# Recurrences' set-up issued in the last chunk of z; first weight chunk split in the first stage, five copies issued in z's second chunk

## The reference

```python
h = _rmsnorm(x, prm['norm_pre_mix'][l])
z = h @ prm['w_in'][l]                      # (rows, 1024) @ (1024, 3740)
(rq, rk, rv, rg, mq, mk, mv, mi, mf, mo, gqkv, ga, gbeta, gg, nq, nkv, ngate) = jnp.split(z, IN_SPLITS, axis=-1)
o_ret, ret_S = _retention(...)              # three recurrences over the prompt
o_ml, ml_C, ml_n, ml_m = _mlstm(...)
gconv, gdn_conv = _causal_dwconv(st['gdn_conv'], gqkv, prm['gdn_conv_w'][l])   # width 4
gq, gk, gv = jnp.split(jax.nn.silu(gconv), 3, axis=-1)
o_g, gdn_S = _gated_delta(...)
```

## Time and profile before

| what | value |
|---|---|
| runs shown | 4123.53 us median of 3 (4115.71 to 4125.43) |
| profiled execution, its own time | 4113.04 us |
| its span | 4111.3 us |
| mean granted TensorE clock | 0.946 |
| busy: PE, DVE, ACT, POOL | 89%, 46%, 31%, 10% |
| matmuls of z, both layers | L565, L569, L570: 433.4, 384.5, 384.1 us busy (pipelined) |

### The profile page before, as it was taken

One profiled execution on the slowest core, in us unless ns is written; L12 is line 12 of the kernel. 1 busy time (PEld: TensorE's weight loads), 2 busy tenths in 40 slices (PEclk: granted clock), 3 DMA queues, 4 the chain that ended last, 5 costly groups with the idle time before them and its releaser, 6 DMA issues. The chain is left out here.

```text
span 4111.3 us, 55178 instructions
## 1 busy us (share of the span) xinstructions
PE 3677.8 (89%) x22004; PEld 3151.8 (77%) x22004; DVE 1908.6 (46%) x3752; ACT 1260.1 (31%) x2863; POOL 411.4 (10%) x287
## 2 busy tenths in 40 slices
PE   5999697698979999999979996967798999999998
PEld 3888587446668999997768885854465799999875
DVE  3234487663444333335541336875533543333345
ACT  2111265452222212124331113645422321121333
POOL 0035101002100000000000550010021100000000
PEclk9999799798989999999989997978898999999999
DMA  7344332306332222255542433332252422222653
GB/s 241 130 145 148 100 110 83 103 7 221 161 123 90 65 75 64 76 189 192 199 156 92 165 129 110 99 96 58 90 213 94 152 64 78 62 78 62 231 180 134
DMA packets 304475, 499.98 MB, mean 122 GB/s; under 512 B 66757, under 2 KB 228325, under 8 KB 299632
## 3 DMA queue, kind: packets, MB, share of 16 engines
q1 hardware_dynamic: 298955, 421.21, 32.1%
q0 software_dynamic: 4608, 67.11, 4.0%
q10 hardware_dynamic: 656, 8.13, 0.6%
HBM read 395.16 MB, written 116.52 MB: 124 GB/s over the span
## 5 line engine op out<-in xcount | busy, mean ns | idle before, releaser
L1042 PE MATMUL ps<-h_hi,fu_hi 128*128 128x344 f32 x2112 | 682.3, 323 | 10.1 <-DVE h_lo L1266 7.3
L1044 PE MATMUL ps<-h_hi,fu_lo 128*128 128x344 f32 x2112 | 677.5, 321 | 0.0
L1043 PE MATMUL ps<-h_lo,fu_hi 128*128 128x344 f32 x2112 | 677.1, 321 | 0.0
L565 PE MATMUL ps<-zi_whi,h_hi 128*128 128x468 f32 (+1 forms) x1152 | 433.4, 376 | 49.6 <-DVE zi_wlo L646 49.6
L1042 PEld LDWEIGHTS ps<-h_hi,fu_hi 128*128 128x128 f32 x2112 | 398.1, 188 | 14.1 <-DVE h_lo L1266 7.8
L1044 PEld LDWEIGHTS ps<-h_hi,fu_lo 128*128 128x128 f32 x2112 | 398.8, 189 | 0.0
L1043 PEld LDWEIGHTS ps<-h_lo,fu_hi 128*128 128x128 f32 x2112 | 398.2, 189 | 0.0
L569 PE MATMUL ps<-zi_wlo,h_hi 128*128 128x468 f32 (+1 forms) x1024 | 384.5, 375 | 0.0
L570 PE MATMUL ps<-zi_whi,h_lo 128*128 128x468 f32 (+1 forms) x1024 | 384.1, 375 | 0.0
L1068 PE MATMUL ps<-fd_whi,fd_fhi 128*128 128x512 f32 x704 | 276.6, 393 | 15.0 <-DVE fd_flo L1283 14.2
L565 PEld LDWEIGHTS ps<-zi_whi,h_hi 128*128 128x128 f32 x1152 | 217.6, 189 | 79.2 <-DVE h_lo L642 50.8
(11 more groups left out here) (624 smaller groups left out, 6736.4 us busy)
## 6 DMA issues: line engine op xcount, KB each, us to landing
w_ahead<-w_ffn_down SPq DMA_DIRECT2D x44, 1024.0 KB, 5.5
z<-zi_z SPq DMA_DIRECT2D x112, 234.0 KB
zi_h<-z SPq DMA_DIRECT2D x64, 384.0 KB, 4.6
f_all<-fu_f SPq DMA_DIRECT2D x44, 516.0 KB, 3.3
w_ahead<-w_ffn_gate SPq DMA_DIRECT2D x44, 512.0 KB, 4.8
w_ahead<-w_ffn_up SPq DMA_DIRECT2D x44, 512.0 KB, 6.1
fd_raw<-w_ffn_down SPq DMA_DIRECT2D x22, 1024.0 KB, 5.7
zi_raw<-w_in SPq DMA_DIRECT2D x24, 936.0 KB, 5.5
```

Source lines behind the costliest of these rows:

```text
L565: nc.tensor.matmul(out, rows_hi, w_hi[:, i % 2, k, c0], start=(k == 0), stop=False)
L1042: nc.tensor.matmul(out, up_hi[f % 2][:, j, k, :], h_hi[:, k, seg], start=(k == 0), stop=False)
L1043: nc.tensor.matmul(out, up_hi[f % 2][:, j, k, :], h_lo[:, k, seg], start=False, stop=False)
L1044: m = nc.tensor.matmul(out, up_lo[f % 2][:, j, k, :], h_hi[:, k, seg], start=False, stop=(k == KD - 1))
```

## The change

1. *First stage.* The four loads of the first weight chunk (first layer only) are issued by SP behind the third tile's store; ScalarE and VectorE make their halves at the end of the stage. `project_in` of the first layer no longer does this (`SPLIT`). For it the weight buffers get fixed places (`PromptEarly`).
2. *Copies.* The five copies leave ScalarE's queue and the first stage; SP issues them in z's second chunk, ahead of the store of tile 11.
3. *Set-up.* All of it moves into z's last chunk (tiles 63 to 71, `FINAL` = 63) in both layers; the first row tile's operands and first rows are loaded there too. The last chunk's tiles use six PSUM banks, the set-up two.
4. *Convolution.* Its steps stand four tiles apart, not five.

```diff
+                    if t == 2:
+                        for k in range(0, KD, 2):
+                            first_weights(sp, io, 0, E, k, S(f"w_first{k // 2}"))
...
-                act.wait_ge(S("row_stored"), 16)
-                norm_stored(kit, act)
-                for h in range(H):
-                    act.dma_start(env["wdist"][h], env["wrow"][h].partition_broadcast(P)).then_inc(env["first_copies"], 16)
-                act.dma_start(x_cur[0:SEQ, :], io["x_prompt"][0]).then_inc(env["first_copies"], 16)
+                for k in range(KD):
+                    if k % 2 == 0:
+                        act.wait_ge(S(f"w_first{k // 2}"), 16)
+                    nc.scalar.activation(E.w_hi[:, k], E.raw[:, k], ACT.Copy).then_inc(S("first_high"), 1)
...
+                for k in range(KD):
+                    dve.wait_ge(S("first_high"), k + 1)
+                    V.tensor_tensor(E.w_lo[:, k], E.raw[:, k], E.w_hi[:, k].bitcast(F32), ALU.subtract)
...
-    conv_in = {29 + 5 * j: j for j in range(NT)}
-    conv_act = {33 + 5 * j: j for j in range(NT)}
-    conv_scale = {34 + 5 * j: j for j in range(NT)}
+    SPLIT = KD if l == 0 else 0
+    conv_in = {29 + 4 * j: j for j in range(NT)}
+    conv_act = {32 + 4 * j: j for j in range(NT)}
+    conv_scale = {33 + 4 * j: j for j in range(NT)}
+    FINAL = (NZ - 1) * TT
...
+        return n % NBK if n < FINAL else (n - FINAL) % 6
...
+                        if l == 0 and n == TT + 2:
+                            first_copies(sp, env, io)
...
+                        if n == FINAL - 1:
+                            sp.wait_ge(S("lo_ready"), KD * NZ - SPLIT)
+                            setup.tables(sp)
+                            for k in range(NZO):
+                                sp.wait_ge(S(f"z_stored{k}"), 16 * len(range(k, FINAL, NZO)))
+                            setup.gate_columns(sp)
+                            sp.wait_ge(S("x_stored0"), 16)
+                            sp.wait_ge(S("z_summed"), FINAL)
+                            setup.first_heads(sp)
+                        if n == FINAL + 5:
+                            setup.rows_out(sp, 0)
+                        if n == FINAL + 6:
+                            setup.rows_back(sp, 0)
+                        if n == FINAL + 7:
+                            setup.rows_out(sp, 1)
+                setup.rows_back(sp, 1)
+                setup.all_in(sp)
...
+                        if n == FINAL + 2:
+                            z_wait(pe, users[6][-1])
+                            setup.pe_sums(pe)
+                        if n == FINAL + 3:
+                            z_wait(pe, users[7][-1])
+                            setup.pe_rows(pe)
+                        if n == FINAL + 4:
+                            setup.pe_max(pe)
+                        if n == FINAL + 5:
+                            setup.pe_ends(pe)
+                        if n == FINAL + 7:
+                            setup.pe_mu(pe)
...
+                    if n == FINAL + 1:
+                        setup.dve_gates(dve, link)
+                    if n == FINAL + 2:
+                        setup.dve_decays(dve, link)
+                    if n == FINAL + 3:
+                        setup.dve_scan(dve, link)
+                    if n == FINAL + 4:
+                        setup.dve_max(dve, link)
+                        setup.dve_shifts(dve, link)
+                    if n == FINAL + 7:
+                        setup.dve_rows(dve, link)
...
+    def pe_sums(self, pe):
+
+        S, T, R, ps = self.kit.sem, self.kit.nc.tensor, self.R, self.env["ps"]
+        pe.wait_ge(S("lf_g"), 1)
...
+    def dve_gates(self, dve, link):
...
+        dve.wait_ge(S("gates_in"), self.ldg.n)
+        dve.wait_ge(S("tables_in"), self.ldc.n)
```

More of the change, by code:

```diff
@@ L142, in program @@
         env = dict(locals())
-        first_stage(kit, env, io, tabs)
+        early = [PromptEarly(nc, l) for l in range(DEPTH)]
+        first_stage(kit, env, io, tabs, early[0])
         kit.next_stage()
         for l in range(DEPTH):
+            E = early[l]
             with ExitStack() as c:
@@ L302, in first_stage @@
         low3 = sb("t_low3", [P, 1], I32)
+        assert nc.sbuf_base <= E.start
         with nc.Block() as b:
@@ L450, in project_in, with bank @@
     A_TILES, V_TILES = (0, 2, 4, 6), (1, 3, 5, 7, SAMPLE)
+    def bank(n):
+        return n % NBK if n < FINAL else (n - FINAL) % 6
+    users = [[n for n in range(NZ * TT) if bank(n) == k] for k in range(NBK)]
     def z_wait(eng, n):
@@ L498, in _ @@
                 load_h(0)
[L499 to L502, removed]
+                for k in range(SPLIT, KD, 2):
+                    first_weights(sp, io, l, E, k, S(f"w_first{k // 2}"))
                 load_h(1)
@@ L557, in _ @@
                             pe.wait_ge(S("h_low"), t + 1)
-                        if n >= NBK:
-                            z_wait(pe, n - NBK)
+                        before = [u for u in users[bank(n)] if u < n]
+                        if before:
+                            z_wait(pe, before[-1])
                         for k in range(KD):
-                            if t == 0:
-                                pe.wait_ge(S("lo_ready"), KD * i + k + 1)
+                            if t == 0 and KD * i + k >= SPLIT:
+                                pe.wait_ge(S("lo_ready"), KD * i + k + 1 - SPLIT)
@@ L618, in _ @@
                 h_high(0)
-                for k in range(KD):
+                for k in range(SPLIT, KD):
                     high(0, k)
@@ L1450, in __init__, with sb @@
         self.fq, self.fk = sb("fq", NT, H), sb("fk", NT, H)
-        def nc_t(name, shape, dt):
-            return nc.sbuf_tensor(name, shape, dt, allow_name_mangling=True)
-        self.scan = ctx.enter_context(nc_t("r_scan", [32, 2, 64 + P], F32))
-        self.rows = ctx.enter_context(nc_t("r_rows", [32, 2, P], F32))
-        self.brow = sb("brow", 2, 2, H, P)
+        self.scan = at("r_scan", [32, 2, 64 + P])
+        self.rows = at("r_rows", [32, 2, P])
+        assert at.at <= self.start + RAW_BYTES
+        at = Place(nc, self.start + RAW_BYTES, l)
+        self.brow, self.zq, self.xq = at("r_brow", [P, 2, 2, H, P]), at("r_zq", [P, 2, 4, 256]), at("r_xq", [P, 2, 8, HD])
+        assert at.at <= TOP
+class PromptTiles:
+    def __init__(self, nc, ctx, states, E):
+        def sb(name, *shape):
+            return ctx.enter_context(nc.sbuf_tensor("r_" + name, [P, *shape], F32, allow_name_mangling=True))
+        self.upper, self.maskT, self.last, self.ones, self.lev, self.lev0T, self.xi = E.upper, E.maskT, E.last, E.ones, E.lev, E.lev0T, E.xi
+        self.rope, self.gains, self.gates, self.zsm, self.qa, self.ends, self.mp, self.ml = E.rope, E.gains, E.gates, E.zsm, E.qa, E.ends, E.mp, E.ml
+        self.fq, self.fk, self.scan, self.rows, self.brow, self.zq, self.xq = E.fq, E.fk, E.scan, E.rows, E.brow, E.zq, E.xq
+        self.Sret, self.Caug, self.Sgdn, self.mprev = states.Sret, states.Caug, states.Sgdn, states.mprev
+        self.vr, self.vm, self.gz = sb("vr", 2, 256), sb("vm", 2, H, HD + 1), sb("gz", 2, 3, 256)
         self.ta, self.tb, self.qk = sb("ta", 8, HD), sb("tb", 8, HD), sb("qk", 2, 8, HD)
@@ L1524, in values_in @@
             ld(R.gz[:, q, j, :], z[r0:r0 + P, a:a + 256])
-    ld = Loads(sp, S("gates_in"))
-    for j, name in enumerate(("mlstm_b_i", "mlstm_b_f", "gdn_dt_bias", "gdn_A_log")):
-        ld(R.gates[:, 4 * j:4 * j + 4], vector(name))
-    ld(R.zsm[:, 0], tiles(MI, 8))
-    ld(R.zsm[:, 1], tiles(GA, 8))
-    ld(R.upper[:], io["c_upper"])
-    heads_in(0)
-    ldc = Loads(sp, S("tables_in"))
-    ldc(R.rope[:], io["c_rope"][0:SEQ].rearrange("(t p) n -> p t n", p=P))
-    ldc(R.xi[:].rearrange("p a h -> p (a h)"), io["c_xi"])
-    ldc(R.last[:], io["c_last"])
-    ldc(R.maskT[:], io["c_maskT"])
-    ldc(R.lev[:].rearrange("p a n -> p (a n)"), io["c_lev"][:, 0:(STEPS + 1) * P])
-    ldc(R.lev0T[:], io["c_levT"][:, 0:P])
-    for j, name in enumerate(("ret_norm", "mlstm_norm", "gdn_norm")):
-        ldc(R.gains[:, j, :], vector(name))
     values_in(0)
@@ L1544, in prompt_sync @@
     values_in(1)
-    for k, ready in enumerate(("decay_rows", "max_rows")):
-        sp.wait_ge(S(ready), 1)
-        sp.dma_start(env["r_rows"][k].rearrange("t (h n) -> (t h) n", h=H), R.rows[:, k]).then_inc(S("rows_stored"), 16)
-    sp.wait_ge(S("rows_stored"), 32)
-    rows_in(0)
-    rows_in(1)
     beside(Loads(sp, env["kept"]))
```

323 lines of the change are left out of this document (206 added, 117 removed).

## The result

The change made the kernel slower: 4161.23 us (4 runs, 4159.6 to 4174.72) against 4121.01 (4 runs, 4115.71 to 4125.43), a ratio of 1.0101, 95% interval 1.0079 to 1.0124, or 33 to 51 us. The direction of the sum was right (+11.5 us), its size was not, and 4161 lies outside the range of 4105 to 4154. The profiled execution of the changed kernel spans 4171.8 us and is the longest of its runs, that of the kernel before (4111.3) is shorter than all of its own; so the two traces are compared stretch by stretch, and what differs in stretches that no edit touches is looked at apart.

A forecast was written before the change was run, and what follows sets the result against it. TensorE, busy 354.95 of 355.00 us, was taken to bound z. Terms 2 x (32 + 10.5 - 26) - 21.5 = +11.5 us gave 4133 on the runs' median basis; forecast 4126 to 4142, whole range 4105 to 4154.

The forecast's parts named there:

- the sum: Whole kernel: 2 x (32 + 10.5 - 26) - 21.5 = +11.5 us, put on record as 4133 us.
- -26 per layer: Head of the recurrences: its 34.13 us shrink to 8 before the first scores; bounds -24.5 to -28.4.
- the 1.5 allowed at the stage's end: End of z: SP's last rows come back behind the last stores, three issues of 0.48, per layer.
- First stage: Start of the first layer's z: first matmul at 69.8 instead of 92.05, taken as -21.5 us, bounds -18 to -22.9.
- the copies at 0: z's second chunk: the moved copies cost 0; the rival that they block it, +10, 4144, had chance 0.02.
- Convolution and set-up in z: Per layer: +32 from TensorE waiting for late splits, +10.5 from the set-up in z's last chunk.
- The chain: Eight convolution steps in z, 22.5 or 25.3 us per cycle against 19.6 for four tiles; last split done at 196.8.
- the third rival's mechanism: Convolution in z: late splits fall into the loads, leaving GpSimd alone and links shorter by 0.5; 4127, chance 0.18.
- the second rival's: Convolution in z: longer links, 7.83 us for each step's loads instead of 7.06, +6.4 per layer; 4148, chance 0.22.
- a stall soon after another adds little: TensorE's half-clock restarts after stalls in z: up to 2.6 us for one, 2.1 allowed for all.
- the single buffer: Convolution in z: one buffer used by all, so step j+1's loads need step j's silu; cycle 22.5 us.
- the 25.3 us of tiles that VectorE empties: Convolution cycle where VectorE empties the gating tile: squares, a split and an emptying come first, 25.3 instead of 22.5.

The follow-up runs named there:

- e1: Changed kernel with SP loading the recurrences' third tile's operands and rows ahead of the sample rows' loads; 1.0040 of the kernel before, against the changed kernel's 1.0101.
- e5: Kernel before with only the first weight chunk's early loads and halves and the copies in z's second chunk; 0.9935 of the kernel before.
- e7: Changed kernel, three of a convolution step's four loads waiting for the addition alone, all issued ahead of their tile's store; 0.9935 of the kernel before.
- e4: Changed kernel, three of a convolution step's four loads waiting for the addition alone, still behind the store in SP's row; 1.0096 of the kernel before.
- the reruns: Kernel before and changed kernel once more, unaltered, for their profiles, one execution each; 4118.12 and 4155.59 us.
- e8: Changed kernel with convolution five tiles apart, third tile's operands ahead of sample loads, set-up steps from sums to shifts one tile later; 0.9888 of the kernel before.
- e2: Changed kernel with the convolution's steps five tiles apart again, as before the change; 0.9970 of the kernel before.

## Why the prediction was wrong, step by step

**The step that failed** is the last term of the change, "-26 per layer" for the recurrences' start. The first scores did come so much earlier against z's end (23.9 in place of 24.5, that is 26 less the 1.5 allowed at the stage's end), and 8.2 us after the recurrences' first instruction, where 8 was taken. But the term took for granted that the whole loop moves with its first scores. SP did not: its loads of values and sample rows start when the recurrences start, and the third tile's operands stand at the end of them. Before, SP issued the values' loads while the set-up still ran, and began the sample rows' 6.4 us ahead of the first scores; the change took that time away and left the queue, so that they now begin 1.0 behind the first scores. 8.5 us per layer come back, 17 in all, and e1 shows it. Without them the result would be some 4144, inside the range. The prediction had no term and no rival for it: it asked what would be late in z, and not what would be late in the loop.

**First stage.** -21.5 predicted, -20.5 measured, the copies at 0: right (e5). SP's last issues came 2.6 later than before (58.32 + 4.07 against 59.80) and the turn took 3.3, while the way from the first load to the first matmul was 5.9 in place of 6.79; the 0.8 allowed for the weights' loads was too little by 1.

**Convolution and set-up in z.** +42.5 per layer predicted with 1.5 of it at the stage's end, so 41 in z; +41.5 measured. The places are right: 16.9 us in tile 54 where 22 was said, 7.5 in tile 63 where 10 was, 5.6 at the sums where 4.9 was. The split of the sum is not.

The chain was shorter. From step 0's loads (222.72) to the end of the last split (416.83) it took 194.1 us where 196.8 was worked out. GpSimd took 11.2 to 11.8 per step instead of 12.1, about 5 less over the eight, which was the third rival's mechanism: the splits now come late, while GpSimd waits for loads. The ways from load to GpSimd took 6.9 to 8.3 where 7.06 was taken, 2.5 more in all, the second rival's. The Trainium skill ("SBUF — State Buffer", section "Who interferes with whom") says that a VectorE instruction with two SBUF inputs contends with GpSimd's reads; this trace agrees, with 11.2 to 11.5 in steps that no split falls beside, and 11.8 to 12.5 in e7, where one to three splits fall beside each step.

The restarts were undercounted. Slow matmuls cost some 11 us in the first layer's z, where before the change it was 2.0 at its start. The guess that "a stall soon after another adds little" holds only in part: the 4 to 5 us of slow matmuls between the waits for splits are covered by the chain, which let TensorE go on at its own time, but another 5 behind the last of these waits and the one at the sums are not, where 2.1 was allowed. So z's delay came out right partly by luck: some 3 us too much for the chain stand against 3 too little for the restarts.

**The chain.** The prediction named the single buffer as what holds the cycle. e4 shows a second hold, which it had taken only as a lengthening (the 25.3 us of tiles that VectorE empties): the loads' place behind a store, in SP's row. e7 takes both away.

**What is left open.** The touched stretches give +31.8 in the first pair of profiles and +29.7 in the reruns; the medians differ by 40, with an interval from 33 to 51. The remaining 8 to 11 us are the size of the attention's lean, whose cause is open. Of the prediction's distance from the result, 40 less 11.5, 17 are the loop, 3 the start, z and the turn, and about 9 this remainder.

## What to carry to other kernels

When a serial stretch is taken out ahead of a loop, look at every queue that used to work during it: here SP used the set-up's time for the values' loads and the first of 33 us of sample loads, behind which the third tile's operands stand, and shortening the stretch by 24 us gave back 8.5. Before a chain is set to a shorter pace, measure its cycle from the same event to the same event, and read in each engine's row what stands ahead of the next link; a load that waits for a store of a tile that is emptied behind the step is part of the cycle, even when its own condition came earlier. Here the remedy was above all the order of a queue (e1, e7); with it, the later set-up steps (e8) and a pace of four and a half, the change is worth 62 us instead of costing 40.

## What the runs showed of the hardware

The seven steps of the scan are small VectorE maxima (32 x 128, both operands in SBUF). They took 2.16 us in the changed kernel, 0.31 each, and 7.30 (e2) and 8.67 (e8) beside a convolution step on GpSimd. In e2 those that ran wholly beside it took 1.84 to 1.89 each, which is the length of one of GpSimd's additions (1.80 to 1.84). GpSimd's step was not longer for it (11.40 in both). Splits, which are larger (128 x 468), do lengthen it: a step took 11.2 to 11.5 us with none beside it, 12.0 to 12.2 with two (e2, e8) and 12.3 to 12.5 with three (e7), so some 0.3 for each, while a split took up to 2.3 in place of 0.57.

TensorE's clock fell in waits and came back after some matmuls. In the changed kernel's first layer, the wait of 14.6 us was followed by nine matmuls 0.39 to 0.56 apart in place of 0.213, the 5.8 by two, up to the next wait of 1.6, that one by ten, and the 5.6 at the sums by thirteen. A wait of about 2 us does not spare it: after the 2.1 in tile 54 TensorE went on at 0.32 and 0.21, waited another 0.2 and then ran slow (0.50 granted from 345.80 to 347.80), and after the 2.4 in e7 the next seven were slow. After the 0.7 in tile 45 only the first was late.

The attention, with equal instructions and nearly equal waits of TensorE, took 259 to 272 us, as the granted clock of the stretch went from 0.84 to 0.78.
